# Reordering the opening of a two-block float32 kernel: rms chain, copy of x to DRAM, k/v chunks, rope tables

## The reference, cut to what matters

```
first_block (two layers l = 0, 1), x and ctx are (1, 256, 2048):
  shift, scale, gate       = split(silu(c)     @ ada_w[l] + ada_b[l], 3)
  shift_c, scale_c, gate_c = split(silu(c_ctx) @ ada_w[l] + ada_b[l], 3)
  h  = rmsnorm(x,   norm_g[l]) * (1 + scale)   + shift
  hc = rmsnorm(ctx, norm_g[l]) * (1 + scale_c) + shift_c
  q, k, v, up, uf, g = split(h @ w_in[l]);  the same of hc
  q, k: rmsnorm per head, rope (x only); attention of 8 heads on 2 k/v heads
  up: pooling by a matrix and a map; uf: a 2-D DFT and a map
  x   = x   + gate   * ((concat(att, pool, fourier) * silu(g)) @ w_out[l])
  ctx = ctx + gate_c * (the same of the context), only for l = 0
second_block: one layer of gated mixing and a linear recurrence, then a feed-forward part
```

## Time and profile before

| What | Value |
|---|---|
| median of 3 runs | 2423.96 us (2416.76 to 2426.70) |
| the profiled execution, its time | 2428.89 us |
| its span in the trace | 2427.1 us |
| granted TensorE clock, mean | 0.978 |
| PE busy (matmul) | 2318.9 us, 96% |
| DVE busy | 1313.9 us, 54% |
| ACT busy | 1045.7 us, 43% |
| POOL busy | 249.5 us, 10% |
| DMA moved | 436.67 MB, mean 180 GB/s |

### The profile page before, as it was taken

One profiled execution on the slowest core, in us unless ns is written; L12 is line 12 of the kernel. 1 busy time (PEld: TensorE's weight loads), 2 busy tenths in 40 slices (PEclk: granted clock), 3 DMA queues, 4 the chain that ended last, 5 costly groups with the idle time before them and its releaser, 6 DMA issues.

```text
span 2427.1 us, 30672 instructions
## 1 busy us (share of the span) xinstructions
PE 2318.9 (96%) x12135; PEld 1860.8 (77%) x12135; DVE 1313.9 (54%) x2113; ACT 1045.7 (43%) x1597; POOL 249.5 (10%) x325
## 2 busy tenths in 40 slices
PE   5889999999999979899999988999999999999998
PEld 2467777677777746678888867888888888888887
DVE  2444533142323255444777876667765777567764
ACT  2222333342322164344554654455543555345543
POOL 1000100000001031100011114111100111001111
PEclk8989999999999989999999999999999999999998
DMA  9864343344655575533556553456655655566552
GB/s 368 288 248 148 137 140 124 110 136 163 219 173 174 174 249 195 192 109 123 189 179 206 169 179 122 161 181 189 194 186 185 189 183 183 190 191 190 191 188 83
DMA packets 347022, 436.67 MB, mean 180 GB/s; under 512 B 13848, under 2 KB 269280, under 8 KB 345984
## 3 DMA queue, kind: packets, MB, share of 16 engines
q1 hardware_dynamic: 341376, 413.19, 51.4%
q0 software_dynamic: 3408, 16.38, 1.9%
q10 hardware_dynamic: 2096, 5.15, 0.6%
HBM read 428.37 MB, written 6.29 MB: 179 GB/s over the span
## 4 chain that ended last, share of the span: by engine, by line
PE 85%; DVE 6%; DMA 3%; ACT 3%; issue 2%; POOL 1%; SPq 0%; ACTq 0%; POOLq 0%; DVEq 0%
PE ps L1205 31%; PE ps L1206 16%; PE ps L1200 5%; PE ps L1202 5%; PE ps L1201 5%; PE ps L1186 4%; PE ps L1188 4%; PE ps L1187 4%; PE ps L1167 3%; DVE SPL L1614 2%; DMA RAW<-in_w_in_dram 2%; ACT SPL L1383 2%; PE ps L1250 1%; PE ps L1267 1%; DMA RAW<-in_ada_w_dram 1%
## 5 line engine op out<-in xcount | busy, mean ns | idle before, releaser
L1205 PE MATMUL ps<-HS,SPL 128*128 128x512 f32 x3456 | 1224.6, 399 | 6.3 <-POOL HS L2086 3.9
L1614 DVE TENSOR_TENSOR SPL<-RAW,SPL 128x1024 fp32r<-128x1024 f32 x592 | 750.4, 1271 | 633.6 <-ACT SPL L1383 631.0
L1206 PE MATMUL ps<-HS,SPL 128*128 128x256 f32 x3456 | 970.2, 281 | 0.0
L1383 ACT ACTIVATE SPL<-RAW 128x1024 fp32r<-128x1024 f32 x592 | 622.1, 1055 | 486.1 <-PE ps L1206 306.2
L1205 PEld LDWEIGHTS ps<-HS,SPL 128*128 128x128 f32 x3456 | 653.4, 189 | 163.2 <-POOL HS L2086 3.4
L1206 PEld LDWEIGHTS ps<-HS,SPL 128*128 128x128 f32 x3456 | 656.9, 190 | 2.0 <-issue 1.9
L1186 PE MATMUL ps<-SPL,HS 128*128 128x512 f32 x576 | 251.6, 437 | 28.2 <-POOL HS L2031 7.8
L1188 PE MATMUL ps<-SPL,HS 128*128 128x512 f32 x576 | 231.0, 401 | 0.0
L1187 PE MATMUL ps<-SPL,HS 128*128 128x512 f32 x576 | 230.7, 401 | 0.0
L1200 PE MATMUL ps<-HS,SPL 128*128 128x512 f32 x512 | 212.1, 414 | 1.2 <-DVE HS L1770 1.2
L1202 PE MATMUL ps<-HS,SPL 128*128 128x512 f32 x512 | 200.4, 391 | 0.0
(11 more groups left out here) (259 smaller groups left out, 1619.9 us busy)
## 6 DMA issues: line engine op xcount, KB each, us to landing
RAW<-in_w_in_dram SPq DMA_DIRECT2D x208, 512.0 KB, 5.7
RAW<-in_ada_w_dram SPq DMA_DIRECT2D x192, 512.0 KB, 4.9
RAW<-in_ffn_w_up_dram SPq DMA_DIRECT2D x192, 512.0 KB, 3.6
RAW<-in_w_out_dram SPq DMA_DIRECT2D x96, 512.0 KB, 4.2
RAW<-in_ffn_w_down_dram SPq DMA_DIRECT2D x96, 512.0 KB, 3.2
x_spill<-XT POOLq DMA_DIRECT2D x2, 2048.0 KB, 14.5
XT<-x_spill POOLq DMA_DIRECT2D x1, 4096.0 KB, 15.9
MM<-in_x_dram ACTq DMA_DIRECT2D x2, 1024.0 KB, 10.8
```

What stands on the lines that cost most here:

```text
L1205: mm(PS[b][:, :], wr, hh, start=k == 0, stop=False, skip_group_check=True)
L1206: m = mm(PS[b][:, 256:512], wl, hh[:, 0:256], start=False, stop=k == KT - 1, skip_group_check=True)
L1383: act(SPL[:, (n - 1) % NSPL, 0, :], raw_of(i), ACT.Copy).then_inc(s_hi, 1)
L1614: tt(w[:, 1, :], raw_of(s["i"]), w[:, 0, :].bitcast(F32), ALU.subtract).then_inc(s_lo, 1)
```

## The change

Five edits, all in the planner; no instruction is added or taken away.

1. `start` returns 8 ada chunks, a k/v chunk, 8 ada chunks, a k/v chunk for u = 1, 2, 3. The k/v chunks become numbers 24, 33, 42, 51, 60, 69, 70, 71.
2. `first_rstd` is cut in two. rstd_a comes behind the second turned tile of x, rstd_b behind the fourth.
3. "spill" no longer waits for chunk 68; it stands as a task of its own behind the 16 turned tiles.
4. At u = 3 the tail of tasks is load_tables, load_dft, idle, idle, tables.
5. The first four chunks of `left` come right behind the last k/v chunk, ahead of the q projection. So every later ada group begins and ends four chunks of `left` earlier, and layer 1's projections hold 20 of them, not 24.

```diff
                 def start_h():
                     after_ada()
-                    if u == 3:
-                        put("spill", last=[multiplied()])
                     hi.extend(staged([tile_h(0, k, s, x, h) for k in range(4 * u, 4 * u + 4) for s in range(2)])
-                              + ([load_tables, tables, load_dft] if u == 3 else []))
+                              + ([load_tables, load_dft, idle, idle, tables] if u == 3 else []))
                 cs[-1].then = start_h
-                return cs[:12] + kv[2 * u - 2:2 * u - 1] + cs[12:] + kv[2 * u - 1:2 * u] if u else cs
+                return cs[:8] + kv[2 * u - 2:2 * u - 1] + cs[8:] + kv[2 * u - 1:2 * u] if u else cs
...
-        lay_out(main0[0] + mixed(main0[1], left))
+        head = main0[0] + left[:4]
+        del left[:4]
+        lay_out(head + mixed(main0[1], left))
...
-        def first_rstd():
-            slot, _ = rstd_a(4, 1.0 / D, STAT, [(s_sqx, 4)])
-            x0["rs"] = rstd_b(4, slot, 5)
+        def first_rstd_a():
+            x0["slot"], _ = rstd_a(4, 1.0 / D, STAT, [(s_sqx, 4)])
+
+        def first_rstd_b():
+            x0["rs"] = rstd_b(4, x0["slot"], 5)
...
-        hi.extend([turn_x(j) for j in range(KT)] + [first_rstd])
+        turns = [turn_x(j) for j in range(KT)]
+        hi.extend(turns[:2] + [first_rstd_a] + turns[2:4] + [first_rstd_b] + turns[4:] + [lambda: put("spill", last=[])])
```

## The result

The changed kernel takes 2432.88 us (median of 10 runs, 2429.19 to 2438.07) beside 2423.19 us for the kernel before: ratio 1.0040, 95% interval 1.0028 to 1.0052, so **9.7 us slower**. The experiments were run in three groups, each beside its own runs of the kernel before, so experiments of different groups are compared by their ratios. The forecast was 2420.4 with a range to 2432; the measurement lies just outside, on the side that had the smaller chance. The profiled execution took 2432.05 us, its span is 2430.2.

A forecast was written before the change was run, and what follows sets the result against it. TensorE bounds the kernel from 180 us; the opening is bound in turn by the DMA rate and a buffer-load-split loop. 2428.9 profiled - 1.1 - 2.5 = 2425.3, median 4.9 lower: 2420.4 us, range 2407 to 2432.

The forecast's parts named there:

- the fifth edit's term: Before q: four ada chunks run free in TensorE's gap, 2.1 us from saved pairs and 1.2 from the clock.
- The opening: Up to q: first k/v chunk at 60.7, spill issued at 58.2, q at 162.2; 1.1 us gained, bounds -6 to +8.
- One turn of the loop: Between k/v chunks: buffer freed, load issued, landed, split, multiplied; 15.1 us for nine chunks, four turns to 138.8.
- Rival 1: Opening: loads land before wanted, nine chunks take 12.0 us, q 12.4 us sooner, 2408 us; chance 0.18.
- the gate of 8 buffers: Opening: k/v chunks nine apart, so a k/v load can't be issued while the k/v chunk before it runs.
- Rival 2: Opening: all matmuls at 1.2 GHz, a k/v chunk takes 10.0 us, a turn 17.5, total 2430 us; chance 0.12.
- Rival 3: Only the opening counts: layer 0's end wins nothing, a slot held in layer 1 takes it back; 2423 us, chance 0.20.
- The second k/v chunk: Opening, chunk 33: load issued at 68.8 crawls beside the spill until 75.1; TensorE starts it at 78.4, bounds 74 to 80.
- the 17 us from the earlier trace: Spill in the opening: 17 us from issue to end, taken from the rows, so over at 75.1 from issue at 58.2.
- The tables: Before q: VectorE still meets them just ahead of rows_out, priced at nothing; GX lands 6 us after issue, at 158.8.
- The end of layer 0: Last ada group ends behind the fourth FILL chunk, removing a 2.00 us wait; 2.5 us gained, bounds 0 and 4.

The follow-up runs named there:

- experiment 1: Changed kernel with one empty item behind the first step of each head-norm chain of layer 0's q projections; 0.9991 of the kernel before, 2426.04 us.
- experiment 2: Changed kernel without its fifth edit, so no four ada chunks ahead of the q projections; 1.0011 of the kernel before, 2427.70 us.
- experiment 5: Changed kernel with the empty item in the head-norm chains of both layers; 0.9980 of the kernel before, 2421.52 us.
- experiment 9: Changed kernel with nine buffers for raw weights in place of eight and three for split ones in place of four; 2435.04 us in one run.
- experiment 7: Kernel before with the even spacing of the k/v chunks alone; 1.0039 of the kernel before, 9.5 us slower.
- experiment 4: Kernel before, with the turns of the two ada groups ending beside layer 0's q projections sent out with the next item; 1.0023, 2431.17 us.
- experiment 3: Kernel before with the fifth edit alone, four ada chunks ahead of the q projections; 1.0040 of the kernel before, 2435.88 us.
- experiment 11: Kernel before with the spill (copy to DRAM) alone moved, behind the rms chain; 0.9981 of the kernel before, 4.6 us faster.
- experiment 6: Changed kernel with the empty item in both layers' head-norm chains and the old k/v chunk spacing; 0.9943 of the kernel before, 2412.57 us.

## Why the prediction was wrong

**The step that failed is the fifth edit's term, and with it the place where its side effect was looked for.** The prediction said of the four ada chunks that they run free in the gap, save two pairs "at places where TensorE is full", give back 1.2 of clock, and let layer 0's last group end under FILL: 2.1 + 1.2 + 2.5 = 5.8 us gained. It followed the moved ends of the ada groups to the end of layer 0 and into layer 1, and not through the q projections between, where they had been holding a gap open. Measured, the edit costs: 1.0040 with it, 1.0011 without, 7 us; alone on the kernel before it costs 9.7. With the gap kept it seems to gain: 0.9991 against 1.0011, 4.9 us, near the 5.8, though the two intervals overlap a little. So the terms that the sum had aren't contradicted, and a term was missing: 12 us by the ratios (1.0040 less 0.9991), 9.3 in the traces between the start of q and the read-back. It had no row before: a wait that an item prevents by its mere place in a list isn't in a trace. It could have been had from the planner's rule by asking, for each group end that moves, what was taken next in the list there.

**The opening** was forecast well. First k/v chunk 59.82 (forecast 60.7), spill issued 57.74 (58.2), q 160.89 (162.2), the wait for VectorE's split ahead of every later k/v chunk 3.4 to 3.7 us (3.5). One turn of the loop: (136.01 - 75.63) / 4 = 15.1, exactly the sum of the prediction; the k/v chunk in it, 90.52 to 98.03, takes 7.5 (7.6). In experiments 1, 2 and 5, which have the same opening up to there, the sixth k/v chunk starts at 137.3 to 138.0, nearer still to the 138.8. Rival 1, that the loads keep up, is out, and experiment 9 shows that the gate of 8 buffers is the reason, though with 9 the rate of the loads stops it at 13.2 us a turn. Rival 2, that the clock never recovers, is out by the same 7.5. Rival 3 looked for a cost of the moved group ends in layer 1 alone.

**The second k/v chunk** was taken at 78.4 and came at 75.63. The spill is the cause. The copy is two DMAs; their issues (KB each, the mean of the two times from issue to landing in us), before and after:

```profile
x_spill<-XT POOLq DMA_DIRECT2D x2, 2048.0 KB, 14.5
```
```profile
x_spill<-XT POOLq DMA_DIRECT2D x2, 2048.0 KB, 11.0
```

The halves land 8.9 and 13.1 us after their issues, in the kernel before 12.0 and 17.1. So the last of it lands at 71.5, 13.7 us after the first issue at 57.74. Its data began within 2 us of the issue and not after 5, and of its 4.19 MB only 0.14 were left from 69 on, so that the load issued at 69.69 shares the engines with next to nothing and lands in 3.5 us; the 17 us from the earlier trace rows were too long for this place. The Trainium skill (DMA: Bandwidth & Descriptors, Anatomy of one DMA, SWDGE path) gave 11.6 us for the copy and a start of the k/v chunk 3 us earlier. The start agrees, 75.63; the copy itself took 2.1 us longer than by the rule, but that is nearer than the row of another stretch.

**The single edits** were priced less well than their sum. The rms chain, spill and tables gain 6.1 us, of it 4.6 from the spill, which had been called worth only what the tables win. The spacing costs 8.7 to 9.5, where the prediction had no price for it alone; its 6.4 for the sixth k/v chunk is net of what the rms chain wins. In the pairs that differ by the spacing alone that chunk starts 7.4 and 7.5 us later (138.02 against 130.63, 137.41 against 129.93). The net of the four edits, experiment 2, is 2.7 us of loss, not clear of noise; the forecast for the same was 162.2 - 159.96 = 2.2. That the two agree so well, with the parts priced as they were, is in part luck.

**The tables** did as foretold: VectorE still meets them ahead of rows_out, now with a wait of 5.25 us on GX in place of 10.36. GX landed some 5.3 us after its issue at 149.08; 6 was taken.

**The end of layer 0:** no wait for ada_out is left in 665 to 860, where 2.0 us stood, and the offset to the kernel before falls from 11.4 us at the read-back to 8.2 at layer 1's first chunk (871.86 against 863.62). The forecast was 2.5. There TensorE now waits 5.4 us for GpSimd's tiles in place of 2.4, and a wait of 1.8 us for ada_out turns up in layer 1, at 889.21. In layer 1 the moved ends took the gap of the head norm too: 10.5 us of waits in place of 3.9, where the prediction had looked only at TMP slots.

What stays open: why experiment 7 costs 9.5 us when its own trace shows q only 6.1 us later, against 9 or more in the other two pairs (its profiled execution took 2429.34 us, 7 under its median, so its trace may show too little); and why the clock fell around the waits in the changed kernel and in experiment 4 and hardly in experiment 3.

## What to carry to other kernels

Where an order is made by a list from which one step is taken per gap, every step is also a spacer: before moving or removing one, ask what stood behind it and whether that was ready a gap earlier. When an edit shifts periodic work by part of a period, go through all places where its ends fall, not only the first and the last. And time the parts of a change one by one: here three edits together won 6 us, the spacing lost 9 and the fifth edit 7. Without the spacing, and with an empty item in the gap that the fifth edit had closed, the kernel is 0.57% faster where the whole change was 0.40% slower.

## What the runs showed of the hardware

**Waits and the clock.** Around the head tiles TensorE waited 0.9 and then 2.3 us, and again 0.9 and 2.3 for the next q projection (6.4 in all), otherwise nearly without a gap. In the changed kernel the granted clock reads 0.91 in 220 to 240 and in 280 to 300, so matmuls ran at 1.2 GHz for a part of them; in the kernel before, without these waits, it reads 1.00. In experiment 4 the same waits go with 0.93 over 215 to 240 and over 280 to 305. But in experiment 3, with 6.3 us of the same waits, both stretches read 1.00. So short waits can bring the clock down, and don't always.

**Two queues on the same DMA engines.** The copy of 4.2 MB from SBUF to DRAM is two DMAs. The second landed 13.1 us after its issue in the changed kernel, 13.8 in experiment 11 and 17.1 in the kernel before: the same copy, beside different loads. While both ran in the kernel before, the copy's queue and the weights' queue had the same number of packets, 47 each in 139 to 141, but 0.77 MB against 0.09: the queue with small packets starved beside the one with large ones.

**Traces and medians.** A profiled execution can lie well off the median: experiment 6's has a span of 2403.0 us, its median is 2412.57, so differences under 5 us are read here from medians, or from single stretches of the trace, and not from two spans.
